# Two output-gate blocks of a hybrid decoder layer computed with tokens on the partitions and turned by DMA

## The chip, the cores and the metric

The kernel runs on one core of a Trainium2 chip. Times are device microseconds; the metric is the time of one execution, as a median over runs. The core has five engines that run side by side, each with a queue in order: TensorE (PE, matmuls, with its weight loads as PEld), VectorE (DVE), ScalarE (ACT), GpSimd (POOL) and SyncE (SP, which here only issues DMAs). They meet through semaphores.

## The reference

One decoder layer on 256 tokens of width 1024, in float32:

```python
h = rms_norm(x, attn_norm)
proj = h @ w_in                       # retention branch and softmax (MoBA) branch
...
y_ret  = o_r @ w_ret_o
y_moba = o_m @ w_moba_o
gates = jax.nn.sigmoid(h @ w_gate + b_gate)
gate_ret, gate_moba = jnp.split(gates, 2, axis=-1)
x = x + (gate_ret * y_ret + gate_moba * y_moba) @ w_out
h = rms_norm(x, ffn_norm)
u = causal_depthwise_conv(h @ w_up, conv_w, conv_b)
u_gate, u_val = jnp.split(u, 2, axis=-1)
x = x + (jax.nn.silu(u_gate) * u_val) @ w_down
```

The change concerns `gate_moba`: 1024 channels, computed as two blocks of 512 columns, GATE_M0 and GATE_M1.

## The kernel before, in words

**Weights.** All weights stream through the core once, as 77 "halves", n = 0 to 76, of 1 MB (128 partitions x 2048 float32). Half n goes to one of four slots (n mod 4). SP issues its load as soon as DVE has finished with the slot's last content. Then ACT copies it rounded to the fast matmul type (`split`, L760, "hi") and DVE subtracts to get the rest (`split`, L1045, "lo"); three matmuls (hi x hi, lo x hi, hi x lo) replace each float32 matmul. A block b of 512 output columns is made of the halves 2b and 2b + 1. ACT's split of half n waits until PE has used half n - 4, and PE waits for DVE's split of n (semaphore `lo_ready`).

**Two forms of a block.** In the channel form (`channel_block`) the weights are stationary and the 256 tokens move: the result has channels on the partitions, and a half is 48 matmuls of 256 columns. In the token form (`token_block`) the activations are stationary and 512 weight columns move: the result has tokens on the partitions, and a half is 24 matmuls of 512 columns. What needs channels on the partitions afterwards is then turned. For the query and key heads, the retention output and the probabilities the kernel does that with DMAs: POOL splits the float32 words into planes of 16-bit words, SP's queue issues DMA transposes of 16-bit words between its weight loads, and DVE (`join_heads`, L1188) or ACT joins the turned words again.

**Order around the change.** It is written out by hand. PE runs ... RET_O0, RET_O1, GATE_M0, GATE_M1, MOBA_O0, MOBA_O1, then OUT. ACT and DVE walk over the same blocks: for each block b they do what `first` holds for b, split half 2b + 4, do what `second` holds, and split half 2b + 5; for b = MOBA_O1 the split of half 42 comes ahead of `first`. GATE_M0 is block 16 (halves 32 and 33), GATE_M1 17, MOBA_O0 18 (36 and 37), MOBA_O1 19 (38 and 39); OUT takes halves 40 to 43.

**From the gates to OUT.** ACT applies the sigmoid with the bias as it reads the gate blocks' banks (`sigmoid_gates`, L846). When MOBA_O0 or MOBA_O1 is summed, DVE runs `gate_moba`: two products with the gates that free the banks (L1275), two additions to `merged` (L1281), and, behind ACT's `merged_high` (L893), two subtractions (L1286). OUT is done in tiles of 12 matmuls: for the first 128 tokens the tiles q = 0 to 3, where q = 0 and 1 use halves 40 and 41 and the first four `merged` slices, and q = 2 and 3 use halves 42 and 43 and the last four. Tile q = 1 writes a bank that MOBA_O1 used, so it waits for `gate_moba`'s products of MOBA_O1.

x is loaded a second time for the residual, into `xs`, by POOL's queue (L426), together with a row of gains.

Of the kernel before, what the change touches and what calls it, by code (L numbers as in the profile page):

```python
# [9 lines left out]
P = 128  # L10
# [24 lines left out]
TOKEN_BLOCKS = (V_R0, V_R1, Q_M0, Q_M1, K_M0, K_M1, V_M0, V_M1, OUT0, OUT1, UP0)  # L35
# [22 lines left out]
def hybrid_layer(nc, x, x_chan0, x_chan1, x_chan2, x_chan3, weights, gain_row_in, cols, ident_in, mask_in, rotary_in, decay_in, out):  # L58
# [9 lines left out]
    with ExitStack() as ctx:  # L68
# [3 lines left out]
        def sem(name):  # L72
# [47 lines left out]
                 for part in (a_hi, a_lo)]  # L120
# [34 lines left out]
                  for part in (area[:, 5120:6144], ys[:, 1024:2048], ys[:, 0:1024], xs[:, 0:1024])]  # L155
        JOIN_ORDER = (0, 2, 3, 1)
# [73 lines left out]
        keys_scaled = sem("keys_scaled")  # L230
        ret_planes_ready = sem("ret_planes_ready")
# [38 lines left out]
        def _(sp):  # L270
# [67 lines left out]
            for n in range(2 * SLOTS, LAST_TURN + 1):  # L338
                sp.wait_ge(lo_ready, n - SLOTS + 1)
                sp.dma_start(raw[n % SLOTS][:, :], weights[n]).then_inc(raw_loaded[n % SLOTS], 16)  # L340
                if n in RET_TURNS:
                    turn_ret(RET_TURNS[n])
                if n in HEAD_TURNS:
                    turn_heads(HEAD_TURNS[n])
                if n in (LAST_TURN - 2, LAST_TURN):
                    turn_pairs(1 - (LAST_TURN - n) // 2)
# [14 lines left out]
        def _(pool):  # L361
# [63 lines left out]
            pool.wait_ge(pairs_joined, 4)  # L425
# [15 lines left out]
        def _(pe):  # L441
# [47 lines left out]
            def token_block(b):  # L489
                for h in range(2):  # L490
                    n = 2 * b + h
                    pe.wait_ge(lo_ready, n + 1)
                    if h == 0:
                        wait_bank_free(b)
                    token_half([block_bank(b, t) for t in range(NT)], n, range(4 * h, 4 * h + 4), h == 0, h == 1)\
                        .then_inc(half_used, 1)

# [134 lines left out]
            channel_block(GATE_M0, h_hi, h_lo, lambda: tail_moba_out(1))  # L632
            channel_block(GATE_M1, h_hi, h_lo)
# [115 lines left out]
        def _(act):  # L749
# [88 lines left out]
            def sigmoid_gates(b, first, bias):  # L838
                act.wait_ge(half_used, 2 * b + 2)
                for j in range(2):  # L840
                    if first == GATE_M0:
                        wait_bank_read(act, RET_O1, 1)
                    for i in range(2):
                        k = 4 * (b - first) + 2 * j + i
                        c = COL_GATE_BIAS + bias + k
# [61 lines left out]
            def up_tok_read(t):  # L907
# [14 lines left out]
                GATE_R1: lambda: sigmoid_gates(GATE_R1, GATE_R0, 0),  # L922
# [8 lines left out]
                GATE_R0: lambda: sigmoid_gates(GATE_R0, GATE_R0, 0),  # L931
            }
            for b in range(OUT0):
# [9 lines left out]
                if b == K_M1:  # L943
                    ret_scale()
                if b == V_M0:
# [82 lines left out]
        def _(dve):  # L1028
# [286 lines left out]
            def h2_low(t):  # L1315
# [23 lines left out]
                RET_O0: lambda: gate_ret(RET_O0),  # L1339
            }  # L1340
            for b in range(OUT0):
# [175 lines left out]
```

## Time and profile before

| | |
|---|---|
| runs (3) | median 458.35 us, 458.07 to 458.42 |
| the profiled execution | 457.5 us, of which the span from first to last instruction is 455.4 |
| TensorE busy | 451.7 us (99%) |
| TensorE weight load busy | 417.7 us (92%) |
| VectorE busy | 318.5 us (70%) |
| ScalarE busy | 258.2 us (57%) |
| GpSimd busy | 46.4 us (10%) |
| granted TensorE clock | 1.000 of full |
| DMA | 202 GB/s mean |

An engine's busy share is over the whole span; matmuls overlap each other by more than half, so that their pace is read from the starts and not from the durations. In a timeline row the first number is the start in the span, the second how long the row (x2: two instructions together) took, and the bracket how long the engine had been idle and for whom it waited.

### The profile page before, as it was taken

What the parts mean: (1) busy time and instruction counts of PE and PEld (TensorE: products, weight loads), DVE (VectorE), ACT (ScalarE), POOL (GpSimd) and SP (SyncE); (2) the same over time, 40 slices, a digit from 0 to 9 for tenths busy, and PEclk for the clock granted to TensorE, in tenths of its full rate; (3) what the DMA queues carried; (4) which work ended last, traced back from release to release, by engine and by line L of the source; (5) the groups of instructions that cost most, each with busy time, mean ns of one, the idle gap of its engine ahead of it and who ended that gap; (6) DMA issues with size and microseconds to landing.
All of it is one profiled execution on the core that took longest, in us unless ns stands there. A gap on an engine that the chain in (4) does not pass through costs nothing.

```text
span 455.4 us, 7647 instructions
## 1 busy us (share of the span) xinstructions
PE 451.7 (99%) x3061; PEld 417.7 (92%) x3061; DVE 318.5 (70%) x391; ACT 258.2 (57%) x364; POOL 46.4 (10%) x43
## 2 busy tenths in 40 slices
PE   9999999999999999999999999999999999999997
PEld 6899999888888999999999888999999999888886
DVE  4789994855689748673469565898888888884423
ACT  6776353055996668324435366677676767573300
POOL 0100000595360021110000000000000000000000
PEclk9999999999999999999999999999999999999999
DMA  8997554259999227995446344435554444547002
GB/s 281 422 416 260 219 191 180 94 190 241 246 269 346 94 94 197 283 331 207 186 186 260 110 184 186 184 142 230 184 184 184 184 184 184 186 168 293 1 0 92
DMA packets 33930, 91.92 MB, mean 202 GB/s; under 512 B 20592, under 2 KB 21488, under 8 KB 24560
## 3 DMA queue, kind: packets, MB, share of 16 engines
q1 hardware_dynamic: 33488, 89.97, 56.9%
q0 software_dynamic: 416, 1.57, 0.9%
q8 instruction: 19, 0.31, 0.3%
q14 instruction: 7, 0.06, 0.0%
HBM read 85.77 MB, written 1.05 MB: 191 GB/s over the span
## 4 chain that ended last, share of the span: by engine, by line
PE 99%; DVE 0%; issue 0%; POOL 0%; POOLq 0%
PE bank L507 18%; PE bank L508 18%; PE bank L509 18%; PE bank L461 5%; PE bank L463 5%; PE bank L462 5%; PE bank L743 4%; PE bank L740 4%; PE bank L741 4%; PE bank L648 2%; PE bank L646 2%; PE bank L647 2%; PE bank L475 2%; PE bank L479 2%; PE bank L485 2%; PE bank L591 1%
## 5 line engine op out<-in xcount | busy, mean ns | idle before, releaser
L1045 DVE TENSOR_TENSOR w_pair<-w_raw,w_pair 128x2048 fp32r<-128x2048 f32 x73 | 167.4, 2307 | 60.1 <-ACT w_pair L760 59.8
L760 ACT ACTIVATE w_pair<-w_raw 128x2048 fp32r<-128x2048 f32 x73 | 138.5, 1921 | 37.2 <-PE bank L743 17.1
L507 PE MATMUL bank<-h_hi,w_pair 128*128 128x256 f32 x512 | 143.8, 281 | 0.0
L508 PE MATMUL bank<-h_lo,w_pair 128*128 128x256 f32 x512 | 143.0, 279 | 0.0
L509 PE MATMUL bank<-h_hi,w_pair 128*128 128x256 f32 x512 | 142.9, 279 | 0.0
L508 PEld LDWEIGHTS bank<-h_lo,w_pair 128*128 128x128 f32 x512 | 96.2, 188 | 0.1
L507 PEld LDWEIGHTS bank<-h_hi,w_pair 128*128 128x128 f32 x512 | 96.2, 188 | 0.1
L509 PEld LDWEIGHTS bank<-h_hi,w_pair 128*128 128x128 f32 x512 | 96.2, 188 | 0.0
L507 PE MATMUL bank<-a_hi,w_pair 128*128 128x256 f32 x192 | 53.9, 281 | 0.0
L508 PE MATMUL bank<-a_lo,w_pair 128*128 128x256 f32 x192 | 53.6, 279 | 0.0
L509 PE MATMUL bank<-a_hi,w_pair 128*128 128x256 f32 x192 | 53.5, 279 | 0.0
L1381 DVE SCALAR_TENSOR_TENSOR area<-area,col 128x256 f32<-128x256 f32 x88 | 37.8, 482 | 16.7 <-ACT area L971 14.2
L461 PE MATMUL bank<-w_pair,h_hi 128*128 128x512 f32 x96 | 37.4, 389 | 0.0
L462 PE MATMUL bank<-w_pair,h_hi 128*128 128x512 f32 x96 | 37.4, 389 | 0.0
L463 PE MATMUL bank<-w_pair,h_lo 128*128 128x512 f32 x96 | 37.4, 389 | 0.0
L507 PEld LDWEIGHTS bank<-a_hi,w_pair 128*128 128x128 f32 x192 | 36.1, 188 | 0.2 <-DVE w_pair L1045 0.2
L508 PEld LDWEIGHTS bank<-a_lo,w_pair 128*128 128x128 f32 x192 | 36.1, 188 | 0.0
L509 PEld LDWEIGHTS bank<-a_hi,w_pair 128*128 128x128 f32 x192 | 36.1, 188 | 0.0
L741 PE MATMUL bank<-w_pair,a_hi 128*128 128x512 f32 x80 | 31.2, 391 | 0.0
L740 PE MATMUL bank<-w_pair,a_hi 128*128 128x512 f32 x80 | 31.2, 390 | 0.0
L743 PE MATMUL bank<-w_pair,a_lo 128*128 128x512 f32 x80 | 24.7, 390 | 0.0
L967 ACT ACTIVATE area<-bank 128x512 f32<-128x512 f32 x20 | 12.0, 602 | 20.7 <-PE bank L509 20.7
(153 smaller groups left out, 606.4 us busy)
## 6 DMA issues: line engine op xcount, KB each, us to landing
w_raw<-weights_dram SPq DMA_DIRECT2D x73, 1024.0 KB, 4.9
w_raw<-weights_dram SPq DMA_DIRECT2D x8, 256.0 KB, 5.0
w_raw<-weights_dram SPq DMA_DIRECT2D x4, 512.0 KB, 8.7
ys<-x_dram SPq DMA_DIRECT2D x2, 512.0 KB, 8.8
xs<-x_dram POOLq DMA_DIRECT2D x1, 1024.0 KB, 5.5
area<-decay_dram SPq DMA_DIRECT2D x1, 768.0 KB, 8.7
out_dram<-ys SPq DMA_DIRECT2D x3, 256.0 KB, 2.0
xs<-x_chan_dram SPq DMA_DIRECT2D x1, 512.0 KB, 6.5
```

Source lines behind the costliest of these rows:

```text
L461: mm(o, s_hi, hi[:, kk, :], start=(first and kk == 0), stop=False)
L462: mm(o, s_hi, lo[:, kk, :], start=False, stop=False)
L463: ins = mm(o, s_lo, hi[:, kk, :], start=False, stop=(last and kk == 3))
L507: mm(o, s_hi, r_hi[:, k, :], start=(k == 0 and m % 2 == 0), stop=False)
L508: mm(o, s_hi, r_lo[:, k, :], start=False, stop=False)
L509: ins = mm(o, s_lo, r_hi[:, k, :], start=False, stop=(k == KT - 1 and m % 2 == 1))
L740: mm(bank[4 + 2 * t + c][:, :], s_hi, hi[:, kk, c, :], start=(k == 0), stop=False)
L741: mm(bank[4 + 2 * t + c][:, :], s_hi, lo[:, kk, c, :], start=False, stop=False)
L743: ins = mm(bank[4 + 2 * t + c][:, :], s_lo, hi[:, kk, c, :], start=False, stop=(c == 1 and t == 1 and kk == 1 and j == DOWN_HALVES - 2))
L760: A(w_parts(n, r)[0], raw[r][:, :], ACT.Copy).then_inc(hi_ready, 1)
L1045: tt(lo, raw[r][:, :], hi.bitcast(f32), ALU.subtract).then_inc(lo_ready, 1)
L1381: ins = stt(out=conv[:, jj, m, :], in0=u_in[:, jj, m, tap:tap + SEQ], scalar=conv_col(4 * m + tap), in1=conv[:, jj, m, :], op0=ALU.mult, o ...
```

## The change

GATE_M0 and GATE_M1 are computed in the token form. ACT copies their banks to SBUF without a sigmoid; POOL splits the words into planes (four copies of 128x1024 16-bit words); SP's queue turns them with four DMA transposes, two behind the load of half 41 and two behind that of half 43; DVE joins the words into `gates` (`join_moba_gates`, two copies for each block); and ACT then applies sigmoid and bias in place (`moba_gates`, four instructions for each block). POOL issues the second load of x behind the first two turns instead of behind the probabilities' joins, since its place is used for gate words in between. `gate_moba` waits for the sigmoids.

```diff
-TOKEN_BLOCKS = (V_R0, V_R1, Q_M0, Q_M1, K_M0, K_M1, V_M0, V_M1, OUT0, OUT1, UP0)
+TOKEN_BLOCKS = (V_R0, V_R1, Q_M0, Q_M1, K_M0, K_M1, V_M0, V_M1, GATE_M0, GATE_M1, OUT0, OUT1, UP0)
...
-            LAST_TURN = 2 * GATE_R1 + 9
+            LAST_TURN = 2 * GATE_M1 + 9
+            MOBA_GATE_TURNS = {2 * GATE_M0 + 9: 0, 2 * GATE_M1 + 9: 1}
+            def turn_moba_gates(q):
+                for t in range(NT):
+                    sp.wait_ge(moba_gate_planes_ready, 2 * q + t + 1)
+                    if q == 0:
+                        sp.wait_ge(unit_made, unit("moba_out1", 1) + 1)
+                    sp.dma_start(moba_gate_turned[q][:, t].rearrange("p w m s -> p (w m) s"),
+                                 moba_gate_planes[q][:, t].rearrange("p w c -> p (w c)"), transpose=True)\
+                        .then_inc(moba_gate_was_turned[q][t], 16)
...
-            pool.wait_ge(pairs_joined, 4)
+            for q in range(2):
+                for t in range(NT):
+                    wait_bank_read(pool, GATE_M0 + q, t)
+                    nc.gpsimd.tensor_copy(moba_gate_planes[q][:, t],
+                                          moba_gate_tok[q][:, t].bitcast(u16).rearrange("p (c w) -> p w c", w=2))\
+                        .then_inc(moba_gate_planes_ready, 1)
+            for t in range(NT):
+                pool.wait_ge(moba_gate_was_turned[0][t], 16)
             pool.dma_start(x_tok, x_view).then_inc(x_again, 16)
...
-            channel_block(GATE_M0, h_hi, h_lo, lambda: tail_moba_out(1))
-            channel_block(GATE_M1, h_hi, h_lo)
+            token_block(GATE_M0, lambda: tail_moba_out(1))
+            token_block(GATE_M1)
...
+            def moba_gates(q):
+
+                act.wait_ge(moba_gates_joined, 2 * q + 2)
+                for k in range(4 * q, 4 * q + 4):
+                    c = COL_GATE_BIAS + KT + k
+                    A(gates[:, k, :], gates[:, k, :], ACT.Sigmoid, bias=col[:, c:c + 1]).then_inc(moba_gates_ready, 1)
...
-                GATE_M0: lambda: (attn_read(1), sigmoid_gates(GATE_M0, GATE_M0, KT)),
-                GATE_M1: lambda: sigmoid_gates(GATE_M1, GATE_M0, KT),
+                GATE_M0: lambda: (attn_read(1), act.wait_ge(pairs_joined, 4),
+                                  copy_block(GATE_M0, lambda t: moba_gate_tok[0][:, t])),
+                GATE_M1: lambda: copy_block(GATE_M1, lambda t: moba_gate_tok[1][:, t]),
...
+                if b in (GATE_M1, MOBA_O0):
+                    moba_gates(b - GATE_M1)
...
+            def join_moba_gates(q):
+                if q == 0:
+                    wait_bank_read(dve, RET_O1, 1)
+                for t in range(NT):
+                    dve.wait_ge(moba_gate_was_turned[q][t], 16)
+                for t in range(NT):
+                    dst = gates[:, 4 * q:4 * q + 4, P * t:P * t + P]
+                    nc.vector.tensor_copy(dst.bitcast(u16).rearrange("p m (s w) -> p w m s", w=2),
+                                          moba_gate_turned[q][:, t]).then_inc(moba_gates_joined, 1)
...
                 dve.wait_ge(half_used, 2 * b + 2)
-                if b == MOBA_O0:
-                    wait_bank_read(dve, GATE_M0, 1)
-                    wait_bank_read(dve, GATE_M1, 1)
+                dve.wait_ge(moba_gates_ready, 4 * (b - MOBA_O0) + 4)
...
-                RET_O0: lambda: gate_ret(RET_O0),
+                RET_O0: lambda: gate_ret(RET_O0), MOBA_O0: lambda: join_moba_gates(1),
...
+                if b == GATE_M1:
+                    join_moba_gates(0)
```

Where the instructions stand now: first ACT, from the split of half 38 to that of half 43 (`w_pair0` to `w_pair3` are the slots' rounded weights, `h_hi<-ys` is `merged_high`). Before:

```order
L760 ACTIVATE w_pair2<-w_raw2 128x2048 [waits half_used,raw_loaded2]
L760 ACTIVATE w_pair3<-w_raw3 128x2048 [waits half_used,raw_loaded3]
L893 ACTIVATE h_hi<-ys 128x512 [waits merged_ready] x2
L760 ACTIVATE w_pair0<-w_raw0 128x2048 [waits half_used,raw_loaded0]
L760 ACTIVATE w_pair1<-w_raw1 128x2048 [waits half_used,raw_loaded1]
L760 ACTIVATE w_pair2<-w_raw2 128x2048 [waits half_used,raw_loaded2]
L893 ACTIVATE h_hi<-ys 128x512 [waits merged_ready] x2
L760 ACTIVATE w_pair3<-w_raw3 128x2048 [waits half_used,raw_loaded3]
```

and in the changed kernel, where line numbers are those of the new file (L791 is `split`, L884 a sigmoid in place, L929 `merged_high`):

```order
L791 ACTIVATE w_pair2<-w_raw2 128x2048 [waits half_used,raw_loaded2]
L791 ACTIVATE w_pair3<-w_raw3 128x2048 [waits half_used,raw_loaded3]
L884 ACTIVATE area<-area,col 128x256 [waits moba_gates_joined]
L884 ACTIVATE area<-area,col 128x256 x3
L929 ACTIVATE h_hi<-ys 128x512 [waits merged_ready] x2
L791 ACTIVATE w_pair0<-w_raw0 128x2048 [waits half_used,raw_loaded0]
L791 ACTIVATE w_pair1<-w_raw1 128x2048 [waits half_used,raw_loaded1]
L884 ACTIVATE area<-area,col 128x256 [waits moba_gates_joined]
L884 ACTIVATE area<-area,col 128x256 x3
L791 ACTIVATE w_pair2<-w_raw2 128x2048 [waits half_used,raw_loaded2]
L929 ACTIVATE h_hi<-ys 128x512 [waits merged_ready] x2
L791 ACTIVATE w_pair3<-w_raw3 128x2048 [waits half_used,raw_loaded3]
```

The eight sigmoids are no longer the read of the banks: the first four stand behind the split of half 39 and ahead of `merged_high` of MOBA_O0, the last four between the splits of halves 41 and 42.

Then DVE, from behind the split of half 39 to the products of MOBA_O1 (`ys<-ys,area` is the addition to `merged`, `h_lo` the subtraction). Before:

```order
L1275 TENSOR_TENSOR area<-bank0,area 128x512 [waits bank_read1,bank_read0,half_used]
L1275 TENSOR_TENSOR area<-bank1,area 128x512
L1281 TENSOR_TENSOR ys<-ys,area 128x512 [waits bank_read0] x2
L1286 TENSOR_TENSOR h_lo<-ys,h_hi 128x512 [waits merged_hi_ready] x2
L1045 TENSOR_TENSOR w_pair0<-w_raw0,w_pair0 128x2048 [waits hi_ready]
L1045 TENSOR_TENSOR w_pair1<-w_raw1,w_pair1 128x2048 [waits hi_ready]
L1045 TENSOR_TENSOR w_pair2<-w_raw2,w_pair2 128x2048 [waits hi_ready]
L1275 TENSOR_TENSOR area<-bank2,area 128x512 [waits half_used]
L1275 TENSOR_TENSOR area<-bank3,area 128x512
```

and in the changed kernel (L1084 is `split`, L1308 a join, L1322 a product with the gates):

```order
L1308 COPY area<-area 128x2x4x128 [waits moba_gate_was_turned01,moba_gate_was_turned00,bank_read1]
L1308 COPY area<-area 128x2x4x128
L1322 TENSOR_TENSOR area<-bank0,area 128x512 [waits moba_gates_ready,half_used]
L1322 TENSOR_TENSOR area<-bank1,area 128x512
L1328 TENSOR_TENSOR ys<-ys,area 128x512 [waits bank_read0] x2
L1333 TENSOR_TENSOR h_lo<-ys,h_hi 128x512 [waits merged_hi_ready] x2
L1084 TENSOR_TENSOR w_pair0<-w_raw0,w_pair0 128x2048 [waits hi_ready]
L1308 COPY area<-area 128x2x4x128 [waits moba_gate_was_turned11,moba_gate_was_turned10]
L1308 COPY area<-area 128x2x4x128
L1084 TENSOR_TENSOR w_pair1<-w_raw1,w_pair1 128x2048 [waits hi_ready]
L1084 TENSOR_TENSOR w_pair2<-w_raw2,w_pair2 128x2048 [waits hi_ready]
L1322 TENSOR_TENSOR area<-bank2,area 128x512 [waits moba_gates_ready,half_used]
```

Two joins stand ahead of the products of MOBA_O0, and two between the splits of halves 40 and 41.

## Rows read from the trace of the kernel before

**Rows 1.** The page: the span, and the shares of the chain that ended last.

```profile
span 455.4 us, 7647 instructions
...
PE 99%; DVE 0%; issue 0%; POOL 0%; POOLq 0%
```

**Rows 2.** Timeline of PE (start us, us): first and last matmul of GATE_M0's first half.

```profile
197.62 0.28 PE L507 MATMUL bank<-h_hi,w_pair 128*128 128x256 f32 x1
...
203.10 0.28 PE L509 MATMUL bank<-h_hi,w_pair 128*128 128x256 f32 x1
```

**Rows 3.** Timeline of PE: two matmuls of Q_M0 and Q_M1, 36 apart.

```profile
86.23 0.39 PE L463 MATMUL bank<-w_pair,h_lo 128*128 128x512 f32 x1
...
94.39 0.39 PE L463 MATMUL bank<-w_pair,h_lo 128*128 128x512 f32 x1
```

**Rows 4.** Timeline of PE: first matmul of OUT, and of its fourth tile.

```profile
245.04 0.40 PE L646 MATMUL bank<-w_pair,h_hi 128*128 128x512 f32 x1
...
253.22 0.40 PE L646 MATMUL bank<-w_pair,h_hi 128*128 128x512 f32 x1
```

**Rows 5.** Timeline of ACT behind the end of GATE_M1, [idle before <-releaser].

```profile
222.84 1.57 ACT L846 ACTIVATE area<-bank,col 128x256 f32<-128x256 f32 x4 [6.02 <-PE bank L509]
224.29 3.73 ACT L760 ACTIVATE w_pair<-w_raw 128x2048 fp32r<-128x2048 f32 x2
235.96 1.24 ACT L893 ACTIVATE h_hi<-ys 128x512 fp32r<-128x512 f32 x2 [7.94 <-DVE ys L1281]
237.10 5.53 ACT L760 ACTIVATE w_pair<-w_raw 128x2048 fp32r<-128x2048 f32 x3
247.57 1.24 ACT L893 ACTIVATE h_hi<-ys 128x512 fp32r<-128x512 f32 x2 [4.94 <-DVE ys L1281]
248.71 1.91 ACT L760 ACTIVATE w_pair<-w_raw 128x2048 fp32r<-128x2048 f32 x1
```

**Rows 6.** Timeline of DVE in the same stretch.

```profile
226.25 4.50 DVE L1045 TENSOR_TENSOR w_pair<-w_raw,w_pair 128x2048 fp32r<-128x2048 f32 x2 [6.71 <-ACT w_pair L760]
234.04 1.29 DVE L1275 TENSOR_TENSOR area<-bank,area 128x512 f32<-128x512 f32 x2 [3.30 <-PE bank L509]
...
239.05 6.70 DVE L1045 TENSOR_TENSOR w_pair<-w_raw,w_pair 128x2048 fp32r<-128x2048 f32 x3 [1.12 <-ACT w_pair L760]
245.66 1.28 DVE L1275 TENSOR_TENSOR area<-bank,area 128x512 f32<-128x512 f32 x2
...
250.65 2.29 DVE L1045 TENSOR_TENSOR w_pair<-w_raw,w_pair 128x2048 fp32r<-128x2048 f32 x1 [1.12 <-ACT w_pair L760]
```

**Rows 7.** Timeline of ACT elsewhere: two bank copies, and four scalings in place.

```profile
145.14 1.08 ACT L785 ACTIVATE area<-bank 128x512 f32<-128x512 f32 x2 [3.69 <-PE bank L463]
...
286.84 2.08 ACT L998 ACTIVATE area<-area,col 128x256 f32<-128x256 f32 x4
```

**Rows 8.** Timeline of DVE: two joins of turned words, at two places.

```profile
123.51 2.26 DVE L1188 COPY area<-area 128x1024 uint16<-128x1024 uint16 x2 [1.30 <-DMA area<-area]
...
142.38 1.39 DVE L1188 COPY area<-xs 128x1024 uint16<-128x1024 uint16 x2
```

**Rows 9.** SP's queue: one pair of transposes; and all eight of L314, to landing.

```profile
121.31 5.50 SPq L314 DMA_TRANSPOSE ys<-ys  x2
...
DMA to landing us min/median/max: 4.0/6.4/8.3
```

**Rows 10.** Line L384: POOL's splits of words, min/median/max ns; then DVE's timeline beside one.

```profile
L384 POOL COPY area<-xs x6: 1035/1588/3107, 98.7 to 131.3; 128x1024 uint16<-128x1024 uint16 x6
...
109.04 2.73 DVE L1045 TENSOR_TENSOR w_pair<-w_raw,w_pair 128x2048 fp32r<-128x2048 f32 x1
```

**Rows 11.** Busy time by window: PE, PEld, DVE, ACT, POOL, PEclk, DMA share, GB/s.

```profile
228.00:240.00 12.00, 12.00 (x105) 12.00 (x104) 7.48 (x9) 4.06 (x5) 0.00 (x0) 1.00 0.47 176
```

**Rows 12.** Timeline of PE at the program's start.

```profile
0.99 3.35 PE L537 MATMUL bank<-w_pair 128*128 128x512 f32 x7 [0.99 <-POOL w_pair L387]
...
5.41 0.63 PE L479 MATMUL bank<-w_pair,a_lo 128*128 128x512 f32 x2
```

More of the change, by code:

```diff
@@ L155, in hybrid_layer @@
                   for part in (area[:, 5120:6144], ys[:, 1024:2048], ys[:, 0:1024], xs[:, 0:1024])]
+        moba_gate_tok = [part.rearrange("p (t d) -> p t d", t=NT) for part in (xs[:, 0:1024], area[:, 3072:4096])]
+        moba_gate_planes = [part.bitcast(u16).rearrange("p (t w c) -> p t w c", t=NT, w=2)
+                            for part in (xs[:, 1024:2048], area[:, 4096:5120])]
+        moba_gate_turned = [part.bitcast(u16).rearrange("p (t w m s) -> p t w m s", t=NT, w=2, m=4)
+                            for part in (area[:, 2048:3072], area[:, 6144:7168])]
         JOIN_ORDER = (0, 2, 3, 1)
@@ L230, in hybrid_layer @@
         keys_scaled = sem("keys_scaled")
+        moba_gate_planes_ready = sem("moba_gate_planes_ready")
+        moba_gate_was_turned = [[sem(f"moba_gate_was_turned{q}{t}") for t in range(NT)] for q in range(2)]
+        moba_gates_joined = sem("moba_gates_joined")
+        moba_gates_ready = sem("moba_gates_ready")
         ret_planes_ready = sem("ret_planes_ready")
@@ L324, in turn_pairs @@
                                  pair_planes[g][j].bitcast(u16), transpose=True).then_inc(pair_was_turned[g][j], 16)
-            LAST_TURN = 2 * GATE_R1 + 9
+            LAST_TURN = 2 * GATE_M1 + 9
+            PAIR_TURNS = {2 * GATE_R1 + 7: 0, 2 * GATE_R1 + 9: 1}
+            MOBA_GATE_TURNS = {2 * GATE_M0 + 9: 0, 2 * GATE_M1 + 9: 1}
             ROUNDS = (HALVES - SLOTS) // SLOTS
+            def turn_moba_gates(q):
[6 more added lines that the diff above has]
+                        .then_inc(moba_gate_was_turned[q][t], 16)
             def turn_ret(t):
@@ L344, in _ @@
                     turn_heads(HEAD_TURNS[n])
-                if n in (LAST_TURN - 2, LAST_TURN):
-                    turn_pairs(1 - (LAST_TURN - n) // 2)
+                if n in PAIR_TURNS:
+                    turn_pairs(PAIR_TURNS[n])
+                if n in MOBA_GATE_TURNS:
+                    turn_moba_gates(MOBA_GATE_TURNS[n])
             with sp.Fori((LAST_TURN + 1) // SLOTS - 1, ROUNDS) as i:
@@ L487, in value_products, with token_block @@
                         ins.then_inc(half_used, 1)
-            def token_block(b):
+            def token_block(b, between=None):
                 for h in range(2):
@@ L496, in token_block @@
                         .then_inc(half_used, 1)
+                    if h == 0 and between:
+                        between()
             def channel_half(banks, n, slot, r_hi, r_lo, h):
@@ L836, in square_heads, with sigmoid_gates @@
                     ins.then_inc(sums_qk, 1)
-            def sigmoid_gates(b, first, bias):
+            def sigmoid_gates(b):
                 act.wait_ge(half_used, 2 * b + 2)
                 for j in range(2):
-                    if first == GATE_M0:
-                        wait_bank_read(act, RET_O1, 1)
                     for i in range(2):
-                        k = 4 * (b - first) + 2 * j + i
-                        c = COL_GATE_BIAS + bias + k
+                        k = 4 * (b - GATE_R0) + 2 * j + i
+                        c = COL_GATE_BIAS + k
                         ins = A(gates[:, k, :], block_bank(b, j)[:, SEQ * i:SEQ * i + SEQ], ACT.Sigmoid,
@@ L930, in _ @@
                 V_M0: lambda: (ret_high(0), ret_high(1)), V_M1: lambda: (scale_keys(1), exps(0)),
-                GATE_R0: lambda: sigmoid_gates(GATE_R0, GATE_R0, 0),
+                GATE_R0: lambda: sigmoid_gates(GATE_R0),
             }
```

2 lines of the change are left out of this document (1 added, 1 removed).

## The prediction

> **What bounds the kernel now.** I read the page first: the span is 455.4 us and the chain that ended last is TensorE for 99% of it [rows 1]. So a change gains only what it takes off TensorE's own stream, and costs whatever makes that stream wait. Next I read TensorE's timeline, for the pace of both forms of a block and for the moments at which it needs things, then ScalarE's and VectorE's timelines from GATE_M1 to OUT, where the change puts its work. The reader is to see there that the two engines idle for some microseconds once per block, but that between the end of MOBA_O0 and the fourth tile of OUT they run back to back.
>
> The profiled execution took 457.5 us, 2.1 more than its span; the median of the runs shown is 458.35, 0.85 above it. I work out a difference in the profiled execution and add it to the median.
>
> **What TensorE saves.** A channel half is 48 matmuls of 256 columns. Its first starts at 197.62 and its last at 203.10, 47 steps, so 0.1166 us a step and 5.60 us a half [rows 2]. A token half is 24 matmuls of 512 columns; 36 of these take 8.16 us, so 0.2267 us a step and 5.44 us a half [rows 3]. A half saves 0.155 us and the four halves of the two gate blocks 0.62 us. This is all that the change takes from TensorE, and it is 0.14% of the time. The same pace is seen in OUT, where 36 steps take 8.18 us [rows 4].
>
> **The clock of events behind it.** OUT began at 245.04 [rows 4]. Counting back two channel blocks of 11.19 us, MOBA_O0 ended at 233.85 and GATE_M1 at 222.66; with the saving these become 233.23 and 222.04, and OUT's first tile can start at 244.42. A tile is 12 steps, 2.72 us, so the second tile is due at 247.14 and the fourth at 252.58.
>
> **GATE_M1's banks and join 0.** ScalarE began to read GATE_M1 0.18 us behind its end (222.84) [rows 5], so now at 222.22. Two plain copies take 1.08 us with the next instruction starting 0.1 us before their end [rows 7], where four sigmoids took 1.45 from start to start [rows 5]. The splits of halves 38 and 39 thus start at 223.2. VectorE began its two 1.96 us behind ScalarE's and took 4.50 [rows 5, 6], so 225.16 to 229.66. There the first two joins follow. Two joins of this size took 1.39 us in one place and 2.26 in another [rows 8]; I take 1.39, since here no copy of POOL runs beside them, and end at 231.05. Four sigmoids in place are nearest to the four scalings in place, 2.08 us [rows 7]; from the banks they took 1.57 [rows 5], which is the other end. They end at 233.2. The products with MOBA_O0 need its end too, and began 0.19 us behind it before (234.04 against 233.85) [rows 6]: now at 233.42. So the first gate block costs nothing, being hidden behind MOBA_O0 on TensorE, with about 0.1 us to spare; every microsecond that join 0 comes later than that is added to all below.
>
> **Join 1, on the path.** From the products of MOBA_O0 the old distances hold: `merged_high` 1.92 us and the split of half 40 3.06 us behind them [rows 5, 6], so ScalarE's split of 40 starts at 236.5 and takes 1.84 (a third of 5.53). VectorE's follows at 238.4 and takes 2.23 (a third of 6.70), to 240.6. Now the joins stand in front: 1.39, to 242.0. ScalarE, which has long split half 41, waits for them, runs four sigmoids (2.08, to 244.1) and only then splits half 42. VectorE splits 41 meanwhile (242.0 to 244.2, hidden) and 42 from 1.96 us behind ScalarE's start, 246.0, to 248.3. Only then come the products of MOBA_O1, which began at 245.66 before [rows 6]: 2.6 us later, on a TensorE that is 0.62 earlier. Queued behind the waiting split of 42 are the products that free the bank of OUT's second tile, the last `merged` subtractions, and the split of half 43.
>
> **What is late on TensorE.** The second tile needs the products, 1.29 us with a tenth for the semaphore: 249.7 against 247.14, a stall of 2.5 us. Three tiles from there would reach the fourth at 255.1. That one needs half 43, whose split ended 7.28 us behind the products' start before (245.66; 250.65 + 2.29) [rows 6], so now at 255.55: another 0.4 us. The fourth tile starts at 255.6 instead of 253.22 [rows 4]. Net: 3.0 us of stall less 0.62 saved, +2.4 us. What lies behind (residual, second norm, transposes) hangs on these tiles and moves along with them.
>
> **The bounds.** With sigmoids at 1.57 us the net is +1.9. With joins at 2.26 both times it is +4.0, since the first has little to spare. The nearest rows for my own choice are those of the same operation with nothing of POOL beside it.
>
> **The turns.** Turn 0 stands on SP's queue behind the load of half 41, which goes out when half 37 is split, about 218.8 (GATE_M0 ends at 222.66 - 11.19 - 0.31 = 211.16, and the distances of the block after it hold: 0.18 + 1.0 + 1.96 + 4.50); the planes are ready by then. A pair occupied the queue for 5.50 us, the second issued 1.24 us or more in; from issue to landing it was 4.0 to 8.3 us [rows 9]. So the second lands by 229.1 at the latest, against 229.66. Turn 1 goes out behind the load of 43, at 230.3, and lands by 239.9, against 240.6. I count nothing, with margins of 0.6 and 0.7 us at the slow end. SP is not needed for its next load before 240.6, so its block of 5.5 us is free.
>
> **POOL.** A split of words took 1.04 us alone and 3.1 at worst [rows 10]. Planes of GATE_M0 are due only when turn 0 goes out, 7 us behind the block; those of GATE_M1 8 us behind. The split of VectorE beside such a copy took 2.73 instead of 2.29 [rows 10]; the new copies fall ahead of VectorE's splits of 36 and 38, so I count nothing, and at worst 0.44 us in each block.
>
> The Trainium skill's GPSIMD Engine Reference (section Key points) says that GpSimd shares its SBUF interfaces with VectorE and contends with VectorE instructions that have two SBUF inputs. The splits are such instructions, and the 2.73 against 2.29 agrees. By this rule four added copies could cost VectorE's splits up to 0.9 us, with which the time would be 461.7; by the rows' order of events they do not meet.
>
> **x's second load.** It moves from the stretch at 199 to about 229. Before it kept TensorE waiting for nothing and its leaving brings nothing. In its new place the DMA engines were 47% busy [rows 11], it shares them with loads 42 and 43 and turn 1, and it is wanted only by the residual at about 255. Cost nothing; if it pushes turn 1 past 240.6, see the first rival.
>
> **Forecast.** 458.35 + 2.4 = 460.8 us. Its own range is 460.2 to 462.4 (the bounds above). About 0.2%, 0.9 us, is what a measurement tells from no change.
>
> **Rivals.** (1) *The turned words land late.* For it: margins below a microsecond at the slow end, and 2.5 MB more or less at once with turn 1 (x, the gains, load 43). Against it: the median landing of 6.4 leaves over 2 us. Each microsecond of lateness goes in fully; with 2 us it is 462.8. (2) *The clock falls in the stall.* The granted clock is 1.00 [rows 11], but TensorE never waits there, so the trace cannot say. At the program's start, behind idle time, seven matmuls of 512 columns took 3.35 us and the faster pace is reached by 5.41, that is some 4.2 us at about half the pace [rows 12]. If the stall brings this back once it costs 2.1 us: 462.9. The Trainium skill's TensorE: Matmul & The Clock Gate (section Part 1: The HAM clock gate) has idle time drop the clock from 2.4 to 1.2 GHz until the engine has been busy again. By that rule, if 2.5 us of idling suffice, the time is this rival's. (3) *The path is shorter than I think, and TensorE never waits.* One mechanism: VectorE and ScalarE take join and sigmoids of the second block inside gaps. It decides at the start of MOBA_O1's products: from 245.2 or before, nothing stalls, and the full 0.62 is left, 457.7 us; up to 245.8 it is no change. For it: ScalarE idles from 242.6 to 247.57 in the old trace, room for four sigmoids. Against it: the split of 42 stands behind them in ScalarE's queue, and the joins they wait for cannot start before 240.6, so 245.8 would need 2.5 us less than the rows give.
>
> **How the numbers follow.** The forecast's case 0.70, late words 0.12, the clock 0.06, hidden 0.12. Range: low end 459.0, below the case's own low by the chance of short sigmoids and partial hiding; high end 463.6, taking in both slower rivals. Slower 0.88 (all but the hidden case), within 0.2% 0.09, faster 0.03, since the most that can be gained, 0.62 us, lies within 0.2%; faster would need something beyond the saving.
>
> **What the changed profile would show.** Token matmuls of the gate blocks 0.227 us apart; joins 1.4 us a pair; the products of MOBA_O1 starting about 248.3; PE idle before OUT's second tile by 2 to 3 us, released by VectorE's products, and again briefly before the fourth; nothing elsewhere; POOL's and SP's new work unseen by anyone. Wrong if TensorE shows no idle time between 244 and 256, if VectorE's joins wait for a DMA, or if the clock is below 1.00 behind the stall.

## The result and the profile after

The changed kernel takes 463.19 us (median of 4 runs, 462.52 to 464.61) against 458.21 (4 runs, 457.64 to 458.42): a ratio of 1.0115, 95% interval 1.0097 to 1.0133. It is slower, as forecast, but by 5.0 us (difference of the medians) and not by 2.4. Repeated on another occasion it took 463.67 (6 runs) against 458.04, ratio 1.0152 (1.0123 to 1.0182); the medians alone give 1.0123, since two of the six runs took 465.70 and 467.49. The profiled execution took 463.16 us; these are its span, its busy TensorE, and the shares of the chain that ended last, from the page:

```profile
span 461.3 us, 7450 instructions
...
PE 453.2 (98%) x2965; PEld 414.5 (90%) x2965; DVE 321.3 (70%) x395; ACT 260.5 (56%) x368; POOL 51.2 (11%) x47
...
PE 86%; DVE 5%; DMA 4%; ACT 2%; SPq 1%; issue 1%; POOL 0%; DVEq 0%; ACTq 0%; POOLq 0%
```

TensorE alone no longer makes the chain [rows 1]: 14% of the steps lie on others. TensorE's timeline says where. Start of GATE_M0, start of MOBA_O0, start of OUT, the last matmul of its first tile, the second tile, and the first matmul of the fourth:

```profile
198.35 0.39 PE L490 MATMUL bank<-w_pair,h_hi 128*128 128x512 f32 x1
...
222.81 0.28 PE L538 MATMUL bank<-a_hi,w_pair 128*128 128x256 f32 x1
...
245.21 0.40 PE L677 MATMUL bank<-w_pair,h_hi 128*128 128x512 f32 x1
...
247.72 0.39 PE L679 MATMUL bank<-w_pair,h_lo 128*128 128x512 f32 x1
251.66 0.47 PE L677 MATMUL bank<-w_pair,h_hi 128*128 128x512 f32 x1 [3.54 <-DVE area L1322]
...
252.75 0.63 PE L677 MATMUL bank<-w_pair,h_hi 128*128 128x512 f32 x1
...
255.84 0.39 PE L679 MATMUL bank<-w_pair,h_lo 128*128 128x512 f32 x1
...
258.79 0.39 PE L677 MATMUL bank<-w_pair,h_hi 128*128 128x512 f32 x1
```

From GATE_M0's start to MOBA_O0's it is 24.46 us; before it was 25.02, from 197.62 [rows 2] to this row:

```profile
222.64 0.28 PE L507 MATMUL bank<-a_hi,w_pair 128*128 128x256 f32 x1
```

So 0.56 us were saved, against 0.62 counted. But OUT starts at 245.21, which is 0.17 later than before [rows 4], because GATE_M0 already started 0.73 late (198.35 against 197.62): TensorE had waited 0.55 us for VectorE's join of the probabilities at 190 us, ahead of the changed blocks. Then comes the gap before the second tile, 251.66 instead of 247.93 (245.21 and 2.72): 3.73 us. (The bracket says 3.54, because it counts from the end of the last matmul, and matmuls at full pace overlap; I give delays by the starts, and call the bracket the profiled stall.) And then, from 252.3, the matmuls are 0.43 us apart until 255.3, where they were 0.227 apart before [rows 3]. The busy times by window show the clock with it (columns as in [rows 11]: PE, PEld, DVE, ACT, POOL, PEclk, DMA share, GB/s):

```profile
248.00:250.00 2.00, 0.11 (x1) 0.00 (x0) 1.98 (x1) 0.00 (x0) 0.00 (x0) 1.00 0.63 266
...
252.00:254.00 2.00, 2.00 (x6) 1.55 (x5) 1.90 (x4) 1.86 (x3) 0.00 (x0) 0.51 0.86 356
254.00:256.00 2.00, 2.00 (x7) 1.58 (x6) 0.89 (x2) 1.18 (x1) 0.00 (x0) 0.64 0.31 127
256.00:258.00 2.00, 2.00 (x11) 1.64 (x10) 1.50 (x1) 0.00 (x0) 0.00 (x0) 1.00 0.00 0
```

The granted clock is 0.51 between 252 and 254 us and 0.64 between 254 and 256, the lower of its two levels (1.2 GHz) for most of that time, after TensorE had stood for 3.5 us. The second and third tile took 7.13 us (251.66 to 258.79) instead of 5.44, which is 1.7 us lost.

What held the second tile up is seen on the two engines that feed it. VectorE from join 0 to the split of half 43 (L1308 a join, L1322 a product with the gates, L1084 a split):

```profile
230.34 1.38 DVE L1308 COPY area<-area 128x1024 uint16<-128x1024 uint16 x2
234.21 1.29 DVE L1322 TENSOR_TENSOR area<-bank,area 128x512 f32<-128x512 f32 x2 [2.49 <-PE bank L540]
...
239.21 2.29 DVE L1084 TENSOR_TENSOR w_pair<-w_raw,w_pair 128x2048 fp32r<-128x2048 f32 x1 [1.11 <-ACT w_pair L791]
243.03 1.39 DVE L1308 COPY area<-area 128x1024 uint16<-128x1024 uint16 x2 [1.54 <-DMA area<-area]
244.31 2.28 DVE L1084 TENSOR_TENSOR w_pair<-w_raw,w_pair 128x2048 fp32r<-128x2048 f32 x1
248.02 2.29 DVE L1084 TENSOR_TENSOR w_pair<-w_raw,w_pair 128x2048 fp32r<-128x2048 f32 x1 [1.43 <-ACT w_pair L791]
250.23 1.28 DVE L1322 TENSOR_TENSOR area<-bank,area 128x512 f32<-128x512 f32 x2
...
255.21 2.29 DVE L1084 TENSOR_TENSOR w_pair<-w_raw,w_pair 128x2048 fp32r<-128x2048 f32 x1 [1.11 <-ACT w_pair L791]
```

Up to 239.21 everything is where the forecast has it, 0.8 us later with the late start: join 0 takes 1.38 us, the products of MOBA_O0 wait for TensorE and not for the gates. The second join is different: VectorE is free at 241.5 and waits 1.54 us for a DMA. ScalarE (L884 sigmoids in place):

```profile
231.75 1.71 ACT L884 ACTIVATE area<-area,col 128x256 f32<-128x256 f32 x4 [4.05 <-DVE area L1308]
...
244.46 1.72 ACT L884 ACTIVATE area<-area,col 128x256 f32<-128x256 f32 x4 [3.47 <-DVE area L1308]
246.08 1.91 ACT L791 ACTIVATE w_pair<-w_raw 128x2048 fp32r<-128x2048 f32 x1
```

Four sigmoids take 1.71 us, less than the 2.08 of the scalings that I took [rows 7]. The split of 42 follows at 246.08, VectorE's at 248.02, the products at 250.23: this is the predicted order, with the DMA wait in front. VectorE's split of half 43, which the fourth tile needs, ended at 257.50 (255.21 and 2.29). So even at the full clock the fourth tile could not have started before about 257.6, against 257.1 by the pace: of the 1.7 us that the slow tiles lost, about 0.5 would have been a wait, and the clock's own price is about 1.2. SP's queue, with the second pair of transposes, and the landing of all four:

```profile
228.25 2.53 SPq L360 DMA_DIRECT2D w_raw<-weights_dram  x2
230.82 8.88 SPq L344 DMA_TRANSPOSE area<-area  x2
```

```profile
DMA to landing us min/median/max: 7.4/8.8/11.3
```

The pair held the queue for 8.88 us and landed up to 11.3 us behind its issue, where 8.3 was the longest seen before [rows 9]. POOL issued the load of x at 229.59, just ahead of it. The page has that load at 10.3 us to landing.

### The profile page after: what moved, and what is told of

Read it like the earlier page. It is cut to its first block, busy times and chain, and to the rows that moved or that the text cites. A ratio compares the mean times of both kernels' runs of the same rounds, so it can differ in the third digit from the quotient of the medians.

```text
span 461.3 us, 7450 instructions
## 1 busy us (share of the span) xinstructions
PE 453.2 (98%) x2965; PEld 414.5 (90%) x2965; DVE 321.3 (70%) x395; ACT 260.5 (56%) x368; POOL 51.2 (11%) x47
## 4 chain that ended last, share of the span: by engine, by line
PE 86%; DVE 5%; DMA 4%; ACT 2%; SPq 1%; issue 1%; POOL 0%; DVEq 0%; ACTq 0%; POOLq 0%
PE bank L538 13%; PE bank L539 13%; PE bank L540 13%; PE bank L491 6%; PE bank L490 6%; PE bank L492 6%; PE bank L774 4%; PE bank L771 4%; PE bank L772 4%; DMA area<-area 4%; PE bank L677 2%; PE bank L679 2%; PE bank L678 2%; DVE w_pair L1084 2%; PE bank L504 2%; PE bank L508 2%
## 5 line engine op out<-in xcount | busy, mean ns | idle before, releaser
L1084 DVE TENSOR_TENSOR w_pair<-w_raw,w_pair 128x2048 fp32r<-128x2048 f32 x73 | 167.5, 2306 | 60.8 <-ACT w_pair L791 60.4
L791 ACT ACTIVATE w_pair<-w_raw 128x2048 fp32r<-128x2048 f32 x73 | 138.5, 1920 | 37.9 <-PE bank L774 17.1
L538 PE MATMUL bank<-h_hi,w_pair 128*128 128x256 f32 x448 | 125.7, 281 | 0.0
L539 PE MATMUL bank<-h_lo,w_pair 128*128 128x256 f32 x448 | 125.1, 279 | 0.0
L540 PE MATMUL bank<-h_hi,w_pair 128*128 128x256 f32 x448 | 125.0, 279 | 0.0
L539 PEld LDWEIGHTS bank<-h_lo,w_pair 128*128 128x128 f32 x448 | 84.2, 188 | 0.1
L538 PEld LDWEIGHTS bank<-h_hi,w_pair 128*128 128x128 f32 x448 | 84.2, 188 | 0.1
L540 PEld LDWEIGHTS bank<-h_hi,w_pair 128*128 128x128 f32 x448 | 84.2, 188 | 0.0
L490 PE MATMUL bank<-w_pair,h_hi 128*128 128x512 f32 x128 | 49.9, 390 | 0.0
L492 PE MATMUL bank<-w_pair,h_lo 128*128 128x512 f32 x128 | 49.8, 389 | 0.0
L491 PE MATMUL bank<-w_pair,h_hi 128*128 128x512 f32 x128 | 49.8, 389 | 0.0
L492 PEld LDWEIGHTS bank<-w_pair,h_lo 128*128 128x128 f32 x128 | 24.0, 188 | 5.0
L490 PEld LDWEIGHTS bank<-w_pair,h_hi 128*128 128x128 f32 x128 | 24.0, 188 | 4.9
## 6 DMA issues: line engine op xcount, KB each, us to landing
xs<-x_dram POOLq DMA_DIRECT2D x1, 1024.0 KB, 10.3
```

What stands on the lines that cost most here:

```text
L490: mm(o, s_hi, hi[:, kk, :], start=(first and kk == 0), stop=False)
L491: mm(o, s_hi, lo[:, kk, :], start=False, stop=False)
L492: ins = mm(o, s_lo, hi[:, kk, :], start=False, stop=(last and kk == 3))
L538: mm(o, s_hi, r_hi[:, k, :], start=(k == 0 and m % 2 == 0), stop=False)
L539: mm(o, s_hi, r_lo[:, k, :], start=False, stop=False)
L540: ins = mm(o, s_lo, r_hi[:, k, :], start=False, stop=(k == KT - 1 and m % 2 == 1))
```

## The experiments

The theory behind the first runs (A) has four terms: 2.4 us by the order of the instructions, less 0.4 by shorter sigmoids; about 1.5 by the late landing; 1.7 by the clock; 0.6 of chance ahead of the change. The kernels of one call ran on the same chip and share their runs of before: 458.04 us (18 runs) for the first four, 458.09 (35 runs) for the others. A difference with a sign (+2.2 us) is worked out from the ratio; the medians give the same within 0.2 us, but for the first and the third run, where both are said.

**The change once more.** No edit.

> The changed kernel once more, to see which parts of its +5.0 us come back. Theory A (four terms: 2.4 us by the order of instructions, 1.5 us because the second pair of turns landed late, 1.7 us of half clock behind the stall, 0.6 us of probabilities' turns that happened to land late, less 0.4 us of shorter sigmoids): +4 to +6 us again, with DVE waiting for a DMA before the second join, PE idle 3 to 4 us before OUT's second tile, and a granted clock under 1.00 for some 4 us behind it; the 0.6 us at the probabilities comes and goes, as it lies ahead of everything that was changed. Theory B (the late landing was chance): DVE does not wait at the second join, and the total is nearer +3.

Measured: 463.67 us, +5.6 by the medians and +7.0 by the ratio. TensorE waited 3.4 us before the second tile, VectorE 1.41 for the DMA at the second join, the granted clock was 0.50 between 252 and 254 us, and TensorE waited 1.2 us at the probabilities. All terms came back, the last larger than in the first trace. Theory B falls: the late landing is no chance. Two of the six runs, 465.70 and 467.49 us at mean granted clocks of 0.992 and 0.989 (the others 0.993 to 0.996), lost 2 to 4 us more; no trace was taken of them, and where they lost it stays open.

**x's load behind both pairs of turns.**

```diff
             for t in range(NT):
                 pool.wait_ge(moba_gate_was_turned[0][t], 16)
+                pool.wait_ge(moba_gate_was_turned[1][t], 16)
             pool.dma_start(x_tok, x_view).then_inc(x_again, 16)
```

> x's second load and the row of gains are issued only when the second pair of gate turns has landed, so that they share the DMA engines with neither. Theory A (the x load made turn 1 late): turn 1 lands in under 9 us instead of 11.3, DVE does not wait at the second join, the products of MOBA_O1 start 1.5 us earlier, PE's stall is 2.2 us instead of 3.7, and if so short a stall leaves the clock alone the total is +2.0 to +2.6 us over before; if the clock falls all the same, +4. Theory B (the weight loads of halves 42 and 43 made it late): the landing stays at 11 us and the total at +5. x is still there in time for the residual at 257 us in both.

Measured: 460.40 us (7 runs, 459.06 to 462.23), ratio 1.0048 (1.0031 to 1.0066), +2.2 us. The landing of the four transposes, and VectorE at the second join:

```profile
DMA to landing us min/median/max: 7.0/7.7/8.5
```

```profile
240.22 2.29 DVE L1085 TENSOR_TENSOR w_pair<-w_raw,w_pair 128x2048 fp32r<-128x2048 f32 x1 [1.12 <-ACT w_pair L792]
242.43 1.53 DVE L1309 COPY area<-area 128x1024 uint16<-128x1024 uint16 x2
...
247.54 2.29 DVE L1085 TENSOR_TENSOR w_pair<-w_raw,w_pair 128x2048 fp32r<-128x2048 f32 x1 [1.42 <-ACT w_pair L792]
249.75 1.28 DVE L1323 TENSOR_TENSOR area<-bank,area 128x512 f32<-128x512 f32 x2
```

No DMA wait is left: the join starts as the split of half 40 ends. So the load of x and the gains was what made the turns late, and the loads of 42 and 43 were not. The stall is now 2.06 us, 2.25 by the starts (251.18 against 246.21, the start of OUT, and 2.72). In the profiled execution the clock fell again:

```profile
251.18 0.76 PE L678 MATMUL bank<-w_pair,h_hi 128*128 128x512 f32 x1 [2.06 <-DVE area L1323]
```

```profile
252.00:254.00 2.00, 2.00 (x6) 1.52 (x6) 1.53 (x3) 2.00 (x3) 0.00 (x0) 0.50 1.00 406
```

That execution took 462.23 us, and one other whose mean granted clock was also 0.996 took 461.25. The five at 1.000 took 459.06 to 460.78, median 459.71: at the full clock this kernel is 1.7 us above before, and the +2.2 has the clock of two executions in it. So the kernel whose stall was profiled at 2.06 us had its clock brought down in 2 of 7 executions, and the change in all ten of its two groups of runs (0.989 to 0.996), with profiled stalls of 3.54 and 3.42 us.

**The stall filled with matmuls.**

```diff
+                        if q == 1:
+                            wait_unit_read(pe, unit("moba_out1", 0))
+                            for _ in range(14):
+                                mm(bank[7][:, :], h_hi[:, 0, 0:P], w_parts(2 * OUT0)[0][:, 0:512], start=True, stop=True)
                         if kh == 0:
                             wait_bank_free(OUT0 + c)
```

> The changed kernel with 14 extra matmuls of 512 columns (3.2 us at full pace) into an unused bank ahead of OUT's second tile; they compute nothing that is used and end before the bank that PE waits for is free. Theory A (1.7 us of the loss is the clock that falls because PE idles): the stall is as long as before but PE is busy in it, the granted clock stays 1.00, and the total falls by 1.5 to 2.0 us to about +3.2 over before. Rival (the slow stretch is something other than PE's idling, such as a throttle by load or by DMA): granted clock 0.5 to 0.6 at 252 to 256 us as in the changed kernel, and the total unchanged or longer.

Measured: 461.72 us (6 runs), ratio 1.0095 (1.0075 to 1.0116), +3.7 by the medians and +4.4 by the ratio; that is 1.95 us below the change of the same call by the medians, 2.6 by the ratios. TensorE's second tile, the last matmul of its third and the first of its fourth, and the busy times:

```profile
251.18 0.50 PE L677 MATMUL bank<-w_pair,h_hi 128*128 128x512 f32 x1 [0.17 <-DVE area L1326]
...
256.56 0.39 PE L679 MATMUL bank<-w_pair,h_lo 128*128 128x512 f32 x1
257.19 0.50 PE L677 MATMUL bank<-w_pair,h_hi 128*128 128x512 f32 x1 [0.24 <-DVE w_pair L1088]
```

```profile
250.00:252.00 2.00, 1.83 (x9) 1.20 (x8) 2.00 (x4) 0.24 (x1) 0.00 (x0) 1.00 0.64 188
252.00:254.00 2.00, 2.00 (x10) 1.65 (x9) 1.62 (x3) 2.00 (x3) 0.00 (x0) 1.00 0.95 397
```

The second tile starts as late as ever, only the wait is now 0.17 us behind useless work, and the granted clock stays at 1.00. The wait at the fourth tile, which the slow tiles had swallowed in the changed kernel, is back: 0.24 us by the bracket and 0.40 by the starts (257.19 against 256.56 and 0.23), where the forecast had 0.4. The clock's fall is thus shown to come from TensorE's idling. Its price is less than the 1.95 us between the medians. From the second tile to the fourth it is 6.01 us here, and was 7.13 and 7.11 in the two traces of the change, so 1.1 us are the clock's. Of the 1.9 us between the spans of this trace and that of the repeated change, 0.86 lie ahead of GATE_M0 (198.97 there, 198.11 here), where this execution did not wait for the probabilities.

**Without the second block's joins and sigmoids.** Left out is the second half of the gates' joining and sigmoids; MOBA_O1 is multiplied with older values. The turns and x's load still run, and VectorE waits for the turns only ahead of the residual.

```diff
-                if b in (GATE_M1, MOBA_O0):
-                    moba_gates(b - GATE_M1)
+                if b == GATE_M1:
+                    moba_gates(0)
...
-                dve.wait_ge(moba_gates_ready, 4 * (b - MOBA_O0) + 4)
+                dve.wait_ge(moba_gates_ready, 4)
...
-                RET_O0: lambda: gate_ret(RET_O0), MOBA_O0: lambda: join_moba_gates(1),
+                RET_O0: lambda: gate_ret(RET_O0),
```

> The changed kernel without the second block's two joins and four sigmoids (the second half of the gates is left out, so MOBA_O1 is multiplied with older values; its turns and the x load still run, and DVE waits for the turns only before the residual). This is the token form with the first block's words and nothing of the second on the path. Theory A (everything but the second block's join and sigmoids is hidden, and they alone make the stall): PE never idles between GATE_M0 and the residual, clock 1.00, total -0.6 us against before (the pace of the token halves), within 0.5 us. Rival (the first block's join and sigmoids, or POOL's and SP's work, also cost): PE waits at OUT's second or fourth tile and the total is 0 to +2 us.

Measured: 457.29 us (12 runs), ratio 0.9986 (0.9974 to 0.9998), -0.64 us. VectorE runs through as in [rows 6]:

```profile
238.77 6.70 DVE L1084 TENSOR_TENSOR w_pair<-w_raw,w_pair 128x2048 fp32r<-128x2048 f32 x3 [1.12 <-ACT w_pair L791]
245.38 1.28 DVE L1322 TENSOR_TENSOR area<-bank,area 128x512 f32<-128x512 f32 x2
```

TensorE never waits for VectorE's work on the gates or the splits here. The saving agrees with the 0.62 us that were counted. The second pair of turns landed late here too (11.1 us at the latest) and nothing felt it, so what the change loses comes onto the path by two joins and four sigmoids.

**ScalarE's split of 42 ahead of the sigmoids** (with x's load as in the second run).

```diff
-                if b in (GATE_M1, MOBA_O0):
-                    moba_gates(b - GATE_M1)
+                if b == GATE_M1:
+                    moba_gates(0)
...
                 if b == MOBA_O1:
                     split(2 * b + 4)
+                    moba_gates(1)
```

> x's load behind both turns as in the run x_later, and ScalarE splits half 42 ahead of the second block's four sigmoids instead of behind them. Theory A (the order on ScalarE keeps VectorE waiting for the split of 42): VectorE's wait of 1.4 us ahead of its split of 42 is gone, the products of MOBA_O1 start 1.4 us earlier than in x_later, PE's stall is about 0.7 us instead of 2.1, the clock stays at 1.00 in every run, and the total is +0.2 to +0.8 us over before (x_later: +2.2). What is left is the join itself (1.4 us of VectorE) less the 0.6 that PE saves. Rival (the products wait for the sigmoids, not for the split): they start no earlier, total as in x_later.

Measured: 458.43 us (12 runs), ratio 1.0008 (0.9994 to 1.0021): +0.4 us, not to be told from no change. VectorE, and TensorE's second tile:

```profile
240.27 2.29 DVE L1086 TENSOR_TENSOR w_pair<-w_raw,w_pair 128x2048 fp32r<-128x2048 f32 x1 [1.12 <-ACT w_pair L792]
242.47 1.57 DVE L1310 COPY area<-area 128x1024 uint16<-128x1024 uint16 x2
243.94 4.47 DVE L1086 TENSOR_TENSOR w_pair<-w_raw,w_pair 128x2048 fp32r<-128x2048 f32 x2
248.33 1.28 DVE L1324 TENSOR_TENSOR area<-bank,area 128x512 f32<-128x512 f32 x2
```

```profile
249.76 0.47 PE L678 MATMUL bank<-w_pair,h_hi 128*128 128x512 f32 x1 [0.59 <-DVE area L1324]
```

VectorE's wait for the split of 42 is gone (243.94 and 4.47 for both splits, then the products at 248.33 instead of 249.75), and the stall is 0.59 us with the clock at 1.00. So 1.4 us of the order term was ScalarE's sigmoids in front of its split; what is left on VectorE is the join.

**Both turns at once, and the join in a gap.** The second pair of turns goes out behind the first; join 1 stands between the additions and the subtractions of MOBA_O0's `gate_moba`; the sigmoids stand behind the split of 42, and x's load behind both pairs, as in the runs above.

```diff
-            MOBA_GATE_TURNS = {2 * GATE_M0 + 9: 0, 2 * GATE_M1 + 9: 1}
+            MOBA_GATE_TURNS = {2 * GATE_M0 + 9: (0, 1)}
...
                 for j in range(2):
                     merge(j)
+                if b == MOBA_O0:
+                    join_moba_gates(1)
                 for j in range(2):
                     low(j)
```

> Both pairs of gate turns are issued behind the load of half 41 (the second no longer waits for the loads of 42 and 43), the second block is joined between gate_moba's additions and subtractions of MOBA_O0, where VectorE idles 1.1 us for ScalarE, its sigmoids stand behind ScalarE's split of half 42, and x's load goes out behind both turns. Theory A (the loss is only the place of join and sigmoids): turn 1 lands by 236 us, VectorE is delayed by 0.3 us at most, PE has no stall of more than 0.3 us between GATE_M0 and the residual, clock 1.00, total -0.2 to -0.7 us against before. Rival (the loads of 42 and 43, now 5 us later behind the turns, come late and PE or ScalarE waits for a weight load; or turn 1 lands after 237): total 0 to +2 us, with ScalarE waiting for a DMA at the split of 42.

Measured: 457.13 us (12 runs, 456.27 to 458.53), ratio 0.9981 (0.9967 to 0.9995): 0.9 us faster than before, and about 6 faster than the change. That is a little more than the 0.2 to 0.7 expected, and more than the 0.62 that TensorE saves; the interval, 0.2 to 1.5 us, holds both. SP's queue, and VectorE:

```profile
221.25 6.50 SPq L344 DMA_TRANSPOSE area<-xs  x2
227.81 2.69 SPq L344 DMA_TRANSPOSE area<-area  x2
230.54 1.43 SPq L360 DMA_DIRECT2D w_raw<-weights_dram  x2
```

```profile
235.41 1.29 DVE L1325 TENSOR_TENSOR area<-bank,area 128x512 f32<-128x512 f32 x2 [2.49 <-PE bank L542]
...
237.81 1.40 DVE L1311 COPY area<-area 128x1024 uint16<-128x1024 uint16 x2
239.10 1.28 DVE L1336 TENSOR_TENSOR h_lo<-ys,h_hi 128x512 fp32r<-128x512 f32 x2
240.41 6.70 DVE L1087 TENSOR_TENSOR w_pair<-w_raw,w_pair 128x2048 fp32r<-128x2048 f32 x3
247.02 1.28 DVE L1325 TENSOR_TENSOR area<-bank,area 128x512 f32<-128x512 f32 x2
```

The second pair is issued at 227.81 instead of 230.82, ahead of the loads of 42 and 43 (230.54) and of x, and has landed by 232.98, when POOL issues x. The join at 237.81 waits for nothing and runs where VectorE stood idle for ScalarE. Nothing of it is felt: from the products of MOBA_O0 to the split of half 40 it is 5.00 us (235.41 to 240.41), and was 5.01 before (234.04 to 239.05) [rows 6], and TensorE has no wait for it. The rival's late weight load did not come about either. This kernel beats both. The earlier turns and the place of the join were not run apart, so what each of the two is worth alone is not shown.

**Only GATE_M0 in the token form.**

```diff
-            token_block(GATE_M1)
+            channel_block(GATE_M1, h_hi, h_lo)
...
-                GATE_M1: lambda: copy_block(GATE_M1, lambda t: moba_gate_tok[1][:, t]),
+                GATE_M1: lambda: (wait_bank_read(act, RET_O1, 1), sigmoid_gates(GATE_M1)),
```

> Only GATE_M0 in the token form with its turns, joins and sigmoids; GATE_M1 in the channel form with the sigmoid on the read of its banks, as before. Theory A: nothing stands on the path, PE saves 0.31 us (two halves of 0.155), clock 1.00, total -0.3 us, within 0.4. Rival (the first block's words cost something that the saving of the whole hides): +0.2 us or more.

Measured: 457.51 us (12 runs), ratio 0.9990 (0.9978 to 1.0001). That is -0.5 us, in the direction of half the saving, but not to be told from no change. The first block's words cost nothing that can be seen. The load of x, issued at 230.03 with weight loads but no turns beside it, took 9.7 us to land.

**The kernel before, x's load alone moved.**

```diff
             pool.wait_ge(pairs_joined, 4)
+            wait_bank_read(pool, GATE_M1, 1)
             pool.dma_start(x_tok, x_view).then_inc(x_again, 16)
```

> The kernel before with nothing changed but x's second load and the gains, which POOL issues behind the read of GATE_M1's banks (about 224 us instead of 199). All theories: no one waits for it, total within 0.3 us of before. Rival (a share of the changed kernel's loss, or a gain, is in the move itself, by what it does to the weight loads at 199 or at 224): a difference of 0.5 us or more either way.

Measured: 457.89 us (12 runs), ratio 0.9998 (0.9987 to 1.0008). The move by itself costs nothing. (It goes out at 226.0 here, 3.6 us earlier than in the changed kernel, and lands in 5.4 us.) It cost 1.5 us where it met the turns.

## Why the prediction was half right

**Right.** The saving (0.62 us counted, 0.56 in the trace, 0.64 without the second block). The hiding of the first block: join 0 took 1.38 us as predicted, and the products of MOBA_O0 waited for TensorE. POOL's copies: they ended at 214.86 and 225.68, ahead of VectorE's splits at 215.10 and 225.93, and each pair of splits took 4.49 us where it had taken 4.50. The place of the loss: OUT's second tile, behind the products of MOBA_O1, with join and sigmoids between the splits. And, nearly, its size as far as it is a matter of order. With the late landing taken away the second tile is 2.25 us late, where I had 2.56 (249.7 against 247.14): four sigmoids took 1.71 us instead of 2.08, nearer to the lower end that I had from the reads of the banks. The wait at the fourth tile is 0.4, as forecast. With the saving that makes 2.0 us instead of 2.4; the executions at the full clock had 1.7. One phrase of the prediction is a slip: from the second tile's start to the fourth's it is two tiles and not three, and the 255.1 is worked out with two.

**Wrong: the step "The turns", where turn 1 "lands by 239.9, against 240.6. I count nothing".** The longest landing of [rows 9], 8.3 us, was taken from turns beside which weight loads ran, but not the load of x and the gains, 1.5 MB on a second queue. The prediction had put that load at about 229, saw the DMA engines 47% busy over twelve microseconds [rows 11], and drew no price from it. The turns landed up to 11.3 us behind their issue, and VectorE waited 1.5 us. Without x's load the step would have held: in the run with x later the pair had landed by 241.80, when POOL issues x, 0.6 us ahead of the join, where the prediction had a margin of 0.7. The row was the wrong one: it averages over twelve microseconds of a trace in which neither the turns nor x's load stood there. In the changed kernel the same stretch is full:

```profile
230.00:234.00 4.00, 4.00 (x36) 4.00 (x35) 1.71 (x3) 1.71 (x4) 1.83 (x2) 1.00 0.91 346
234.00:238.00 4.00, 4.00 (x37) 4.00 (x36) 3.70 (x6) 1.87 (x3) 0.00 (x0) 1.00 1.11 394
238.00:242.00 4.00, 4.00 (x37) 4.00 (x36) 2.38 (x2) 2.99 (x2) 0.00 (x0) 1.00 0.99 253
```

The last but one column, the DMA engines' share, is 0.91 or more throughout (one value is above 1, so it is a rough measure). Over the twelve microseconds of [rows 11], 228 to 240, it is 0.93 instead of 0.47.

**Wrong: the clock as a rival at 6 in 100.** Its chance was too low: I treated the two rivals as separate. But the late words lengthen the stall from 2.1 to 3.5 us, and with the longer stall the clock came down each time. So the likely cases were the forecast alone (460.8) and forecast with both (464), and hardly anything between. Even the stall that I had forecast, 2.56 us by the starts, is longer than the 2.25 us at which the clock fell in 2 of 7 executions. Its price was too high: I took 2.1 us from the start of the program and added them to a sum that already held the wait of 0.4 us at the fourth tile. The slow tiles lost 1.7 us and swallowed that wait, which leaves 1.1 to 1.2.

**Luck.** The measured 463.19 us lies just inside the range that ends at 463.6. That is no support for the forecast's own sum, which ended at 462.4: the range was widened for two rivals of 0.12 and 0.06 taken one at a time, and both came together.

**Chance.** The profiled execution had 0.73 us more before GATE_M0 than the one before, 0.6 of it a wait for the turned probabilities. This wait is not there in the first trace of before and in two others, and was 0.3 to 1.8 us in seven, 1.0 in that of before with only x later; the join that it waits for was changed by no run. As far as these ten traces show it spreads both kernels' runs and is no part of the change.

The sum over the profiled execution to OUT's fourth tile: 0.79 late at the start of OUT against the forecast clock, -0.62 saved, +3.73 of stall, +1.69 of slow tiles: 5.6, and the trace has 258.79 - 253.22 = 5.57. Of the stall 1.5 us are the late landing (3.73 against 2.25 with x later) and the rest the order. The span is 5.9 longer; 0.3 us of that I did not place.

## What to carry to other kernels

When work is moved to an engine that is idle on average, write its queue out over the stretch where it is needed and ask what stands behind the new instruction: here four sigmoids cost nothing by themselves, and 1.4 us because a weight split stood behind them. When a transfer is moved, price its meeting with the transfers already there at their moments and not from a share averaged over a stage, and treat a longer stall and a fall of TensorE's clock as one case. A saving of 0.14% leaves no room for any of this: it paid only once every added step had a gap of its own.

## What the runs showed of the hardware

- The mean granted clock fell to 0.996 or less in 2 of 7 executions of the kernel with a profiled stall of 2.06 us, in 10 of 10 of the kernel with 3.4 to 3.5 us, and in none of 12 with 0.59 us (the stall was profiled once or twice for each kernel, the clock read in every execution). While it stood at the lower level, matmuls of 512 columns were 0.43 us apart instead of 0.227, for some 3 us. Useless matmuls in the gap kept it at 1.00.
- A pair of DMA transposes that shared the DMA engines with a 1.5 MB load from another queue landed 11.1 to 11.3 us behind issue at the latest in four traces (three kernels), and with that load moved away within 8.5 and 8.6 in two. The 1 MB part of the load itself took 10.3 to 10.6 us in those four; it took 9.7 us with weight loads and no transposes beside it, and 5.4 and 5.5 us in two traces of the kernel before.
- Four in-place sigmoids of 128x256 on ScalarE took 1.71 us, less than four in-place scalings (2.08) [rows 7], which had a scale per partition as well as a bias.
